# Norm chain of a four-layer decoder trunk: one float32 broadcast instead of two parts, and the pre-norm's broadcast one weight unit later

## The reference, cut to what matters

```python
def rms_norm(x, g):
    xf = x.astype(jnp.float32)
    y = xf * lax.rsqrt(jnp.mean(xf * xf, axis=-1, keepdims=True) + EPS)
    return (y * g.astype(jnp.float32)).astype(x.dtype)

def half_ffn(x, g_pre, g_post, w_in, w_out):
    gate, up = jnp.split(rms_norm(x, g_pre) @ w_in, 2, axis=-1)
    return x + 0.5 * rms_norm((jax.nn.silu(gate) * up) @ w_out, g_post)
...
        xp = xp + rms_norm(yp, g[3])
```

## Time and profile before

| what | value |
|---|---|
| median of 3 runs | 2374.9 us |
| runs | 2373.54 to 2384.54 us |
| profiled execution, span | 2375.1 us |
| profiled execution, its own time beside the span | not given on the page; the median of the runs is 0.2 us below the span |
| TensorE matmul busy | 2213.7 us, 93% |
| VectorE busy | 1457.4 us, 61% |
| ScalarE busy | 941.8 us, 40% |
| GpSimd busy | 158.0 us, 7% |
| mean granted TensorE clock | 0.955 |

### The profile page before, as it was taken

How to read it: one execution, slowest core, us unless ns; L and a number is a source line. 1 busy time by engine, 2 the same in 40 slices (tenths; PEclk the granted TensorE clock), 3 DMA queues, 4 the chain that set the end, 5 groups by cost and what they waited for, 6 DMA issues and landing times.

```text
span 2375.1 us, 41971 instructions
## 1 busy us (share of the span) xinstructions
PE 2213.7 (93%) x17475; PEld 2129.9 (90%) x17475; DVE 1457.4 (61%) x1727; ACT 941.8 (40%) x1111; POOL 158.0 (7%) x214
## 2 busy tenths in 40 slices
PE   7999989999999979899999999779999999998997
PEld 6999989998998945789989998468999999898997
DVE  5665866646655567366656645655664665686663
ACT  3443344444434335244344434324443444433442
POOL 3001010001001000010010001001000000101000
PEclk9999999999999989889999999979999999898998
DMA  6554445553554434245545554414554555354550
GB/s 204 177 196 142 160 144 163 185 201 125 177 195 136 161 113 142 89 142 178 188 131 178 186 188 141 143 45 127 183 189 149 166 185 187 118 178 133 185 188 28
DMA packets 286121, 370.76 MB, mean 156 GB/s; under 512 B 12247, under 2 KB 212360, under 8 KB 285924
## 3 DMA queue, kind: packets, MB, share of 16 engines
q1 hardware_dynamic: 282378, 364.57, 46.0%
q10 hardware_dynamic: 3610, 4.28, 0.5%
HBM read 364.87 MB, written 8.11 MB: 157 GB/s over the span
## 4 chain that ended last, share of the span: by engine, by line
PE 56%; DVE 5%; POOL 1%; issue 1%; ACT 0%; ACTq 0%; DVEq 0%; POOLq 0%
PE ps L1371 15%; PE ps L1373 15%; PE ps L1372 15%; PE ps L1423 1%; PE ps L1424 1%; PE ps L1427 1%; PE ps L1677 1%; POOL rs L609 1%; PE ps L1590 1%; DVE kt_dec L1176 1%; DVE probs L1123 1%; PE ps L1547 1%; PE ps L1580 1%; PE ps L1379 1%; PE ps L1390 1%
## 5 line engine op out<-in xcount | busy, mean ns | idle before, releaser
L1371 PE MATMUL ps<-x_hi,w_high_ring 128*128 128x264 f32 x3112 | 893.8, 287 | 0.0
L860 DVE TENSOR_TENSOR w_low_ring<-wstage,w_high_ring 128x2048 fp32r<-128x2048 f32 x332 | 728.4, 2228 | 262.7 <-ACT w_high_ring L630 184.2
L1373 PE MATMUL ps<-x_hi,w_low_ring 128*128 128x264 f32 x3112 | 889.2, 286 | 0.0
L1372 PE MATMUL ps<-x_lo,w_high_ring 128*128 128x264 f32 x3112 | 888.2, 285 | 0.0
L1372 PEld LDWEIGHTS ps<-x_lo,w_high_ring 128*128 128x128 f32 x3112 | 592.8, 190 | 0.0
L1371 PEld LDWEIGHTS ps<-x_hi,w_high_ring 128*128 128x128 f32 x3112 | 591.3, 190 | 0.8 <-issue 0.2
L1373 PEld LDWEIGHTS ps<-x_hi,w_low_ring 128*128 128x128 f32 x3112 | 591.5, 190 | 0.0
L1371 PE MATMUL ps<-h_hi,w_high_ring 128*128 128x264 f32 x1664 | 474.4, 285 | 4.1 <-issue 4.1
L1373 PE MATMUL ps<-h_hi,w_low_ring 128*128 128x264 f32 x1664 | 474.9, 285 | 0.0
L1372 PE MATMUL ps<-h_lo,w_high_ring 128*128 128x264 f32 x1664 | 473.2, 284 | 0.0
L630 ACT ACTIVATE w_high_ring<-wstage 128x2048 fp32r<-128x2048 f32 (+2 forms) x172 | 307.1, 1816 | 311.6 <-PE ps L1373 299.7
(11 more groups left out here) (287 smaller groups left out, 1898.5 us busy)
## 6 DMA issues: line engine op xcount, KB each, us to landing
wstage<-in_ffn_w_in_dram SPq DMA_DIRECT2D x352, 512.0 KB, 5.0
wstage<-in_ffn_w_out_dram SPq DMA_DIRECT2D x160, 512.0 KB, 4.6
wstage<-in_conv_w_in_dram SPq DMA_DIRECT2D x48, 512.0 KB, 4.9
wstage<-in_nsa_w_in_dram SPq DMA_DIRECT2D x20, 512.0 KB, 4.8
wstage<-in_ffn_w_out_dram SPq DMA_DIRECT2D x32, 256.0 KB, 3.3
wstage<-in_conv_w_out_dram SPq DMA_DIRECT2D x16, 512.0 KB, 4.8
wstage<-in_cache_nsa_dram SPq DMA_DIRECT2D x16, 512.0 KB, 4.6
wstage<-in_diff_w_in_dram SPq DMA_DIRECT2D x16, 512.0 KB, 4.9
```

The costliest lines, as they stand in the source:

```text
L860: V.tensor_tensor(w_low_ring[:, u % RING, 0:n, 0:cols], wstage[:, stage_of["w", u] % RING, 0:n, 0:cols], w_high_ring[:, u % RING, 0:n, 0:c ...
L1371: MM(out, wh, hi, start=first, stop=False)
L1372: MM(out, wh, lo, start=False, stop=False)
L1373: return MM(out, wl, hi, start=False, stop=last)
```

## The change

For every norm: the tokens are split in three parts of 88 (`NT`) instead of 128, 128 and 8. The variance is one VectorE instruction instead of two. GpSimd takes the power alone; rounding and difference, `rs_hi`, `rs_lo` and `ident_r` are gone. The broadcast is three float32 matmuls with `rs` and `ident` instead of six with reduced operands.

For the pre-norm alone: statistics and broadcast use spare columns of group 0's banks (504 to 506; 320 to 495 of the first bank and 320 to 407 of the second) instead of group 1's fourth bank, and tile 3 waits for no copy. The broadcast comes behind the whole first unit of group 1 (48 matmuls). VectorE copies `r_pre` in two pieces, and both ScalarE and VectorE split one unit more (the first of group 2) ahead of that.

```diff
-            return 4 * s.outs[1].set if norm % 2 else 4 * s.ins[1].set + 3
+            return 4 * s.outs[1].set if norm % 2 else 4 * s.ins[0].set
+        def stat_col(norm):
+            return 0 if norm % 2 else 504
+        def bcast_out(norm, k):
+            b = norm_bank(norm)
+            if norm % 2:
+                return ps[:, b, 8 + NT * k:8 + NT * k + NT]
+            return ps[:, b + k // 2, 320 + NT * (k % 2):320 + NT * (k % 2) + NT]
...
-                pool.wait_ge(var_ready, 2 * norm + 2)
-                nc.gpsimd.tensor_tensor(rs[:, :], var[:, :], minus_half[:, 0:3], ALU.pow).then_inc(rs_ready, 1)
-                pool.wait_ge(rs_ready, 3 * norm + 1)
-                nc.gpsimd.tensor_copy(rs_hi[:, :], rs[:, :]).then_inc(rs_ready, 1)
-                pool.wait_ge(rs_ready, 3 * norm + 2)
-                nc.gpsimd.tensor_tensor(rs_lo[:, :], rs[:, :], rs_hi[:, :].bitcast(F32), ALU.subtract)\
-                    .then_inc(rs_ready, 1)
+                pool.wait_ge(var_ready, norm + 1)
+                nc.gpsimd.tensor_tensor(rs[0:NT, :], var[0:NT, :], minus_half[0:NT, 0:3], ALU.pow).then_inc(rs_ready, 1)
...
-                    split_to(s.ins[0].end + 2)
+                    split_to(s.ins[0].end + 3)
                     ffn_drain(gates0 + 1, pieces0 + 1, slice(0, 2))
...
-                V.tensor_copy(r_pre[:, :], ps[:, norm_bank(2 * s.i), 8:8 + T]).then_inc(rstd_ready, 1)
-                dve.wait_ge(rstd_ready, s.i + 1)
+                b = norm_bank(2 * s.i)
+                V.tensor_copy(r_pre[:, 0:2 * NT], ps[:, b, 320:320 + 2 * NT]).then_inc(rstd_ready, 1)
+                V.tensor_copy(r_pre[:, 2 * NT:T], bcast_out(2 * s.i, 2)).then_inc(rstd_ready, 1)
+                dve.wait_ge(rstd_ready, 2 * (s.i + 1))
...
                 norm_var(pre)
-                split_to(s.ins[0].end + 2)
+                split_to(s.ins[0].end + 3)
                 norm_copy(s)
...
-                pe.wait_ge(rs_ready, 3 * (norm + 1))
-                b = norm_bank(norm)
-                for tt, (t0, n) in enumerate(TOK):
-                    out = ps[:, b, 8 + t0:8 + t0 + n]
-                    MM(out, rs_hi[0:n, tt:tt + 1].broadcast_to([n, P]), ident_r[0:n, 0:n], start=(tt == 0), stop=False,
-                       skip_group_check=True)
-                    mm = MM(out, rs_lo[0:n, tt:tt + 1].broadcast_to([n, P]), ident_r[0:n, 0:n], start=False, stop=True,
-                            skip_group_check=True)
+                pe.wait_ge(rs_ready, norm + 1)
+                for k in range(3):
+                    mm = MM(bcast_out(norm, k), rs[0:NT, k:k + 1].broadcast_to([NT, P]), ident[0:NT, 0:NT],
+                            start=(norm % 2 == 1 and k == 0), stop=True, skip_group_check=True)
                 mm.then_inc(bcast_done, 1)
...
                         for tile in range(GT):
-                            if tile == 1:
-                                norm_bcast(2 * s.i)
...
-                            if tile == GT - 1:
-                                pe.wait_ge(rstd_ready, s.i + 1)
                             for c in range(HC):
                                 mm = products(4 * g.set + tile, u, c, tile, x_hi[:, c, :], x_lo[:, c, :], c == 0, False)
+                        mm.then_inc(unit_used, 1)
+                        norm_bcast(2 * s.i)
+                        continue
```

More of the change, by code:

```diff
@@ L59 @@
 TOK = [(0, P), (P, P), (SEQ, DEC)]
+NT = T // 3
 def lam_init(layer):
@@ L174, in trunk_kernel @@
         ident = place("ident", [P, P])
-        ident_r = place("ident_r", [P, P], F32R)
         ident_b = place("ident_b", [P, P], BF16)
@@ L192, in trunk_kernel @@
         rs = place("rs", [P, 3])
-        rs_hi = place("rs_hi", [P, 3], F32R)
-        rs_lo = place("rs_lo", [P, 3], F32R)
         minus_half = place("minus_half", [P, 32])
@@ L536, in _ @@
             copy(ident_b[:, :], ident[:, :])
-            copy(ident_r[:, :], ident[:, :])
             select(tmp[:, 0, 0:P], [[-1, P]], ALU.is_ge, NEG, 0, 1)
@@ L902, in norm_var @@
                 dve.wait_ge(stats_done, norm + 1)
-                b = norm_bank(norm)
-                V.tensor_scalar(var[:, 0:2], ps[:, b, 0:2], EPS, None, ALU.add).then_inc(var_ready, 1)
-                V.tensor_scalar(var[0:DEC, 2:3], ps[0:DEC, b, 2:3], EPS, None, ALU.add).then_inc(var_ready, 1)
+                b, col = norm_bank(norm), stat_col(norm)
+                V.tensor_scalar(var[0:NT, :], ps[0:NT, b, col:col + 3], EPS, None, ALU.add).then_inc(var_ready, 1)
             def norm_copy(s):
                 dve.wait_ge(bcast_done, 2 * s.i + 1)
-                V.tensor_copy(r_pre[:, :], ps[:, norm_bank(2 * s.i), 8:8 + T]).then_inc(rstd_ready, 1)
-                dve.wait_ge(rstd_ready, s.i + 1)
+                b = norm_bank(2 * s.i)
+                V.tensor_copy(r_pre[:, 0:2 * NT], ps[:, b, 320:320 + 2 * NT]).then_inc(rstd_ready, 1)
+                V.tensor_copy(r_pre[:, 2 * NT:T], bcast_out(2 * s.i, 2)).then_inc(rstd_ready, 1)
+                dve.wait_ge(rstd_ready, 2 * (s.i + 1))
             def low_x(s, c):
@@ L950, in take_small @@
                 dve.wait_ge(small_loaded, 128)
-                dve.wait_ge(consts_ready, 7)
+                dve.wait_ge(consts_ready, 6)
                 V.tensor_tensor(lam_p[:, :, :], lam_in[:, 0:4:2, :], lam_in[:, 1:4:2, :], ALU.mult).then_inc(lam_summed, 1)
@@ L1375, in norm_stats @@
             def norm_stats(norm, squares, first=True, last=True):
-                b = norm_bank(norm)
-                for tt, (t0, n) in enumerate(TOK):
-                    mm = MM(ps[0:n, b, tt:tt + 1], squares[:, t0:t0 + n], mean_col[:, 0:1], start=(first and tt == 0),
-                            stop=last, skip_group_check=True)
+                b, col = norm_bank(norm), stat_col(norm)
+                for k in range(3):
+                    mm = MM(ps[0:NT, b, col + k:col + k + 1], squares[:, NT * k:NT * k + NT], mean_col[:, 0:1],
+                            start=(norm % 2 == 1 and first and k == 0), stop=last, skip_group_check=True)
                 if last:
@@ L1450, in _ @@
             pe.wait_ge(x_updated, NC)
-            pe.wait_ge(consts_ready, 7)
+            pe.wait_ge(consts_ready, 6)
             def turn_small():
```

## The result

Median 2318.8 us of 4 runs (2317.25 to 2322.61), against 2374.5 for the kernel before on the same chip (4 runs, 2373.54 to 2384.54): ratio 0.977 [0.974, 0.980], 55.7 us less. The forecast was 2324.6, the range 2309 to 2340. The profiled execution took 2318.9, its span is 2317.2, so the two spans differ by 57.9.

What follows compares the result with a forecast made beforehand. TensorE was busy 93% of the span, leaving its waits and low clock to win. 2375.1 - 31.3 (hold) - 13.5 (clock) - 9.6 (post-norm) + 3.9 (convolution) = 2324.6 us, range 2309 to 2340.

Steps and rivals of the forecast that it cites:

- term 1: Pre-norms: TensorE's hold for GpSimd goes because the broadcast stands behind 48 products; 31.3 us less, bounds 29 to 33.
- term 2: Behind five pre-norm broadcasts: TensorE's clock no longer falls once the hold is gone; 13.5 us less, bounds 0 and 13.5.
- Term 3: Post-norms: shorter chain of variance, power and broadcast, all on the path; 0.8 us each, 9.6 us less in twelve.
- more comes back: Rival: some of eleven slow-clock stretches behind the post-norms shorten, 1.7 us and up each; 2300 to 2316, chance 0.12.
- Term 4: Two convolution sublayers: the later copy of the scales makes TensorE wait 1.75 and 2.15 us; 3.9 us given back.
- first rival: The clock falls anyway, the convolution waits being about as long as the holds; 2338 without the clock gain, chance 0.12.
- rival of the late power: Norms: GpSimd's power slips behind VectorE's low parts, or the broadcast costs more than 0.80; 2333 to 2348, chance 0.10.

Runs made afterwards that it cites:

- first experiment: Changed kernel with the rounding and difference on GpSimd kept in the 3x88 layout and six reduced-operand broadcast matmuls: median 2321.1 us, ratio 0.978 against the kernel before.
- second experiment: Changed kernel with the pre-norm broadcast back behind group 1's first tile and one unit less split ahead: median 2345.3 us, ratio 0.988 against the kernel before.
- eight matmuls: Kernel before plus eight unused float32 matmuls of 128 columns ahead of the first sublayer's last input group: 2377.5 us, ratio 1.0015.
- shifted kernel: Changed kernel plus eight unused float32 matmuls ahead of the first sublayer's last input group: 2323.0 us, ratio 0.979 against the kernel before.

## Why the prediction was right, and where not

**Terms 1 and 2, holds and clock: right, 44.4 us against 44.8.** In six sublayers without a fall 14.98 to 15.01 from group 1's start to group 2's became 12.42. That is 2.58 a norm, with the first norm's longer hold some 32 us in all for 31.3 forecast; the other 12 are the clock, for 13.5. The float32 broadcast was over-priced, 0.70 to 0.71 from product to product for 0.80 taken. Its records come 0.11 apart, and so do those of the reduced six, with 88 columns (first experiment) as with 128 (before). So neither the type nor the columns set the pace here; that the weight load does is likely, and no run changes it alone. Behind a wait both take 0.69 from the first record to the next product (245.48 to 246.17 in the first experiment, 242.41 to 243.10 in the second), without one the float32 three take 0.58. The old 0.90 holds two gaps of about 0.2 around its last pair, the one for the 8 tokens (247.77 to 247.97, 248.10 to 248.28). By the Trainium skill's four passes ("FP8 and Floating Point Precision", TensorE Precision Notes) the sum would, as an estimate, have been 2330; the rows side against that price at 88 columns.

All five falls went with the holds. The second experiment shows the tie: with a hold left the clock falls behind it in eight of twelve sublayers, with none in none. Which holds are followed by a fall is not theirs alone to say: the eight matmuls, put into the kernel before, left the holds as they were and made these stretches 7.4 us longer. One premise of term 1 failed without harm: the power was to end 3.3 us behind group 1's start as before, and ended at 5.45. The hold went only because the broadcast asks at 5.90.

**Term 3, post-norm chain: right mechanism, wrong parts, 9.6 a little too small.** The rounding and the difference are 0.53, as priced, in all twelve. The statistics were priced at 0.06 and gave 0.35 in the eight FFN sublayers and 0.15 in the other four, the largest miss of this term. The broadcast was priced at 0.15 and gave 0.04 to 0.07 where both kernels had the same clock. The single variance instruction was priced at 0.06 and gave nothing: from the last statistics record to the power it is 0.49 both times. These sum to 0.93 and about 0.75 a norm, 10.4 us in twelve. The profiled executions have 10.0 in eleven gaps and 1.1 at the end; behind the gaps group 0 ran 2.0 faster, in the slow stretches that the rival "more comes back" spoke of. Those 2 us are the clock.

**Term 4: the waits right, the clock behind them left out.** 1.75 and 2.15 were forecast, 2.04 and 2.12 came, at the place named. But 3.1 us more went in clock falls right behind. The prediction had the rows for it: it priced falls behind waits of 2 us in term 2 and named these very waits in its first rival, but only the wait went into the sum. The sentence that the extra low part "fills the idle 2.32 us and costs nothing" was right that TensorE pays nothing in the FFN sublayers. But VectorE still idles 2.00 ahead of the copy, and the part is no filler: it is what pays for the later copy (31.6 us slower without it).

**The rival of the late power** came half true. (Its price of 0.4 to 1 us in 12 to 24 norms makes 2329 to 2349, not 2333 to 2348.) In eleven of twelve pre-norms the power lost to both low parts and was ready at + 5.45, for the + 5.5 worked out, and was covered by 0.45. The Trainium skill ("SBUF — State Buffer", Who interferes with whom) has an exclusive lock by order of issue. The lock agrees: 0.86 alone, 2.84 to 2.86 behind one low part, 5.04 behind two. The order does not, as far as the rows show it: by it the power, there at 237.20, would have gone ahead of the second low part, which begins at some 239.3. It did so only in the first pre-norm (2.84, with two low parts back to back as well), there also in four variants of the changed kernel with the same order (2.84 to 2.85), and not in the kernel before with the extra part (5.06). Nothing in the rows tells why there. The measurement decides.

**Not in the prediction at all:** 7.2 us less in the attention layers, and the shift of 1.8 us moves the larger of them by as much. Against the profiled span the forecast was 7.4 too high: 7.2 here, 3.9 more gain at term 3, 3.4 and 0.4 less at terms 4 and 1. So the match to 0.3% is partly two misses that cancel, and some 7 us of the 56 are where the clock happened to fall, not work that the change took away.

**The two halves of the change.** By the medians -29 us are the chain and columns and -26 the place with its extra low part. The profiled execution of the second experiment is 33.4 shorter than that of before: post-norms and group 0 behind them 14.0, pre-norms 8.6, attention 8.5, end 2.1. So of the 29 some 8 are clock again. What decides whether a given hold is followed by a fall stays open; only that the falls lie behind TensorE's waits and move with a shift is shown.

## What to carry to other kernels

When a wait goes because its consumer is moved later, look at what that engine's queue does behind it: here one more low part ahead of the copy decided between 56 us won and 24. And when a new wait of about 2 us is forecast for TensorE, price the clock behind it (1.5 us here) with it, as a chance and not as a certainty. A small operation of GpSimd between large two-input operations of VectorE can be given its turn by a semaphore: 0.97 us of VectorE bought 4.2 of GpSimd's. Here that paid together with the earlier broadcast that it allows; on top of the variant with the first groups split further ahead it gained nothing.

## What the runs showed of the hardware that was not expected

- GpSimd's power of 3 columns took 0.86 us with VectorE idle, 2.84 to 2.86 beside one low part of 2.25 and 5.04 to 5.06 beside two back to back, in eleven of twelve pre-norms of the changed kernel and in all twelve of the old layout with the extra part. In the first pre-norm of the changed kernel it got in between the two; when the rounding followed it there, that took 1.44 beside the second low part and 0.18 without one.
- A shift of 1.8 us early in the program changed the attention of layer 1, some 660 us later, by 7.4 us in one kernel (granted clock from 0.82 to 0.88) and by 3.2 the other way in the other (0.88 to 0.84). Two variants cannot be told apart by a profile of each at that size.
- Waits of TensorE of 2.1 us at group 3 were followed by the clock's lower level in both convolution sublayers of the changed kernel (0.81 over 9 us, 1.5 to 1.6 us lost); with 1.2 us it stayed at 1.00. In the shifted kernel and in the one with the two parts, one wait of the same 2.1 had no fall behind it each, and behind eight waits of 2.66 us in FFN sublayers (without the extra low part) there was one fall. Waits of 4.3 us (5.6 in the first) in the pre-norms of the kernel before with the extra part had a fall behind all twelve. So the length alone does not decide.
